# NSA's attention values: four heads at once, split values stationary, output transposed, probabilities scaled on GpSimd

## What is computed

```python
# per chunk of 128 tokens; 8 heads in 2 groups of R = 4; one group shares its keys and values
p_c = masked_softmax(q @ k_cmp - slope * dist)          # 31 compressed blocks
o_c = p_c @ v_cmp
s_s = q @ ks - slope * dist ; p_s = masked_softmax(s_s) # 8 blocks of 64 = all causal keys here
o_s = p_s @ vs
s_w = q @ kw - slope * dist ; p_w = masked_softmax(s_w) # window of 256
o_w = p_w @ vw
gc  = sigmoid(gate_logits)
o   = gc[0] * o_c + gc[1] * o_s + gc[2] * o_w
```

## Time and profile before

| | |
|---|---|
| median of 3 runs | 1001.13 us (1000.83 to 1001.33) |
| the profiled execution | 1001.37 us |
| its span in the trace | 999.5 us |
| PE busy in the span | 977.0 us (98%) |
| DVE, ACT, POOL busy | 568.5, 410.9, 141.4 us |
| NSA's attention slots | from 101.96 to 223.83 us |

### The profile page before, as it was taken

How to read it: one execution, slowest core, us unless ns; L and a number is a source line. 1 busy time by engine, 2 the same in 40 slices (tenths; PEclk the granted TensorE clock), 3 DMA queues, 4 the chain that set the end, 5 groups by cost and what they waited for, 6 DMA issues and landing times.

```text
span 999.5 us, 12861 instructions
## 1 busy us (share of the span) xinstructions
PE 977.0 (98%) x4869; PEld 812.6 (81%) x4869; DVE 568.5 (57%) x1162; ACT 410.9 (41%) x752; POOL 141.4 (14%) x185
## 2 busy tenths in 40 slices
PE   6999999999999999999999999999999999999998
PEld 5778788998888888888777788888888888888887
DVE  5747888863565885646555553575556556522113
ACT  5346555544246554445666433432232232221110
POOL 3000000010002112222434230022111112100000
PEclk9999999999999999999999999999999999999999
DMA  6512110103222211322101234222232223223222
GB/s 232 213 48 79 44 43 2 43 5 114 94 84 85 84 45 62 108 85 85 52 35 42 85 120 161 77 108 84 85 119 92 85 96 115 84 88 124 85 85 85
DMA packets 13693, 86.38 MB, mean 86 GB/s; under 512 B 1472, under 2 KB 1984, under 8 KB 4288
## 3 DMA queue, kind: packets, MB, share of 16 engines
q1 hardware_dynamic: 13632, 85.55, 23.7%
HBM read 83.44 MB, written 2.10 MB: 86 GB/s over the span
## 4 chain that ended last, share of the span: by engine, by line
PE 85%; DVE 8%; ACT 4%; issue 3%; DMA 1%; SPq 0%; DVEq 0%; ACTq 0%
PE ps L1429 22%; PE ps L1431 22%; PE ps L1430 22%; PE ps L1614 7%; PE ps L1457 3%; PE ps L1585 3%; DVE wl L938 2%; DVE prob L1148 1%; PE ps L1569 1%; PE ps L1570 1%; ACT prob_f L804 1%; DVE prob_f L1148 1%; PE ps L1484 1%; DVE pt_l L1170 1%; DMA x<-x 1%
## 5 line engine op out<-in xcount | busy, mean ns | idle before, releaser
L938 DVE TENSOR_TENSOR wl<-raw,wh 128x512 fp32r<-128x512 f32 (+2 forms) x118 | 172.0, 1462 | 130.6 <-ACT wh L644 129.0
L644 ACT ACTIVATE wh<-raw 128x2048 fp32r<-128x2048 f32 (+1 forms) x58 | 109.4, 1886 | 151.0 <-PE ps L1431 132.0
L1429 PE MATMUL ps<-aT_h,wh 128*128 128x512 f32 (+1 forms) x376 | 146.7, 390 | 0.9 <-DVE aT_l L947 0.9
L1430 PE MATMUL ps<-aT_l,wh 128*128 128x512 f32 (+1 forms) x376 | 146.4, 389 | 0.0
L1431 PE MATMUL ps<-aT_h,wl 128*128 128x512 f32 (+1 forms) x376 | 146.3, 389 | 0.0
L1429 PE MATMUL ps<-wh,aT_h 128*128 128x512 f32 x256 | 102.2, 399 | 0.0
L1431 PE MATMUL ps<-wh,aT_l 128*128 128x512 f32 x256 | 100.1, 391 | 0.0
L1430 PE MATMUL ps<-wl,aT_h 128*128 128x512 f32 x256 | 99.8, 390 | 0.0
L1429 PEld LDWEIGHTS ps<-aT_h,wh 128*128 128x128 f32 (+1 forms) x376 | 70.0, 186 | 16.6 <-issue 1.1
L1431 PEld LDWEIGHTS ps<-aT_h,wl 128*128 128x128 f32 (+1 forms) x376 | 70.0, 186 | 15.2
L1430 PEld LDWEIGHTS ps<-aT_l,wh 128*128 128x128 f32 (+1 forms) x376 | 70.0, 186 | 15.1
(11 more groups left out here) (234 smaller groups left out, 1774.2 us busy)
## 6 DMA issues: line engine op xcount, KB each, us to landing
raw<-wblk SPq DMA_DIRECT2D x72, 1024.0 KB, 4.8
x<-x SPq DMA_DIRECT2D x4, 512.0 KB, 5.5
w_sb<-w SPq DMA_DIRECT2D x1, 2048.0 KB, 9.2
hid<-x SPq DMA_DIRECT2D x1, 2048.0 KB, 9.0
out<-outt SPq DMA_DIRECT2D x8, 256.0 KB, 2.1
stage<-consts SPq DMA_DIRECT2D x1, 708.5 KB, 4.7
later<-consts SPq DMA_DIRECT2D x1, 448.0 KB, 5.4
par<-params SPq DMA_DIRECT2D x1, 204.5 KB, 8.6
```

The costliest lines, as they stand in the source:

```text
L644: nc.scalar.activation(wh[b % 2][:, 0:n], raw[b % RING][:, 0:n], ACT.Copy).then_inc(hi_ready, 4)
L938: ins = nc.vector.tensor_tensor(wl[b % RING][:, cols], raw[b % RING][:, cols], wh[b % 2][:, cols].bitcast(f32), ALU.subtract)
L1429: nc.tensor.matmul(dst, a_h, b_h, start=start, stop=False)
L1430: nc.tensor.matmul(dst, a_h, b_l, start=False, stop=False)
```

## The change

The 64 units of NSA are put in another order: by tile and group of four heads, four slc units and then four win units. Such four units share their values, so 128 keys of all four are handled in one step (kind, tile, group, key block); there are 38 steps.

- The probabilities live in a ring of 12 buffers (`prob_n`). DVE works out the coefficients for two units at a time, and GpSimd scales the probabilities in place before they are transposed.
- A step "TA" transposes the key block of four heads into one PSUM bank (four transpositions, as many as before in all). ACT writes the high part (`ptn_h`, 128x512), DVE the low part (`ptn_l`, 128x512). In place of these, the copies of probabilities out of PSUM and the sums into `otok` are gone.
- A step "VA" multiplies split values (`vn_hl`: high and low side by side, stationary) with the high and then the low part of the probabilities, moving, 512 columns each. It accumulates into one bank for each tile and group, into which the compressed part ("OC") writes first.
- "OX" adds the two halves of the bank (ACT copies one, DVE adds in two instructions), "OY" splits the tile's sum into `oT_h` and `oT_l`. The transpositions "OT" of NSA are gone.
- The compressed probabilities are split as well (`pcT`, `vc_hl`), and the values' low parts are written by DVE when the values are projected.

```diff
-        return [(k, h, 0, i) for i in range(TT) for h in range(8) for k in ("slc", "win")]
+        return [(k, 4 * g + r, 0, i) for i in range(TT) for g in range(2) for k in ("slc", "win") for r in range(4)]
+STEPS = [(q, kb) for q in range(16) for kb in range(group_of(q)[3])]
+PT_RING = 3
+P_RING = 12
-    t_lag, o_lag = {NSA: (2, 3), DIFF: (3, 5), FOX: (3, 5)}[m]
+    t_lag, o_lag = {NSA: (3, 7), DIFF: (3, 5), FOX: (3, 5)}[m]
...
+        for q in range(16):
+            kind, g, i, blocks = group_of(q)
+            end = 4 * q + 3
+            put(4 * q + 2, "C", 4 * q + 1)
+            put(4 * q + 4, "C", 4 * q + 3)
+            if kind == "slc":
+                put(end + t_lag + 1, "OC", i, g)
+            for kb in range(blocks):
+                n = STEPS.index((q, kb))
+                put(end + t_lag + kb, "TA", n)
+                put(end + t_lag + 2 + kb, "VA", n)
+            if kind == "win":
+                put(end + t_lag + 2 + blocks, "OX", i, g)
+                if g == 1:
+                    put(end + t_lag + 3 + blocks, "OY", i)
... ACT
+                    elif what == "TA":
+                        full(act, ("TA", j))
+                        if j >= PT_RING:
+                            step_read(act, j - PT_RING)
+                        nc.scalar.activation(ptn_h[j % PT_RING][:, :], ps[b][:, :], ACT.Copy).then_inc(ptn_hi, 1)
... DVE
-                                link(nc.vector.tensor_scalar(coef[:, j:j + 1], rl[:, j:j + 1], gsm[:, i, gi:gi + 1], None, ALU.mult))
+                                nc.vector.tensor_tensor(coef[:, j - 1:j + 1], rl[:, j - 1:j + 1], gsm[:, i, gi - 1:gi + 1], ALU.mult).then_inc(coef_ready, 1)
+                    elif what == "TA":
+                        dve.wait_ge(ptn_hi, j + 1)
+                        nc.vector.tensor_tensor(ptn_l[j % PT_RING][:, :], ps[b][:, :], ptn_h[j % PT_RING][:, :].bitcast(f32),
+                                                ALU.subtract).then_inc(psum_free[b], 1)
-                            nc.vector.scalar_tensor_tensor(dst, ps[b][:, 0:HD], coef[:, j:j + 1], dst, ALU.mult, ALU.add).then_inc(psum_free[b], 1)
... GpSimd
+            for j, u in enumerate(units_of(NSA)):
+                p = scores_at(NSA, j, span(u)[1])
+                pool.wait_ge(coef_ready, j // 2 + 1)
+                nc.gpsimd.tensor_scalar(p, p, coef[:, j:j + 1], None, ALU.mult).then_inc(pn_scaled, 1)
... PE
+                    elif what == "TA":
+                        if kb == 0:
+                            pe.wait_ge(pn_scaled, 4 * q + 4)
+                        transposes(("TA", j), [prob_n[(4 * q + r) % P_RING][:, kb * P:(kb + 1) * P] for r in range(4)])
+                    elif what == "VA":
+                        pe.wait_ge(ptn_hi, j + 1)
+                        nc.tensor.matmul(bk[:, :], v, ptn_h[j % PT_RING][:, :], start=False, stop=False)
+                        free(pe, ("TA", j))
+                        ins = nc.tensor.matmul(bk[:, :], v, ptn_l[j % PT_RING][:, :], start=False, stop=j in ENDS)
```

More of the change, by code:

```diff
@@ L93, in span, with group_of @@
     return s0, (i + 1) * P - s0
+def group_of(q):
+    kind, h, c, i = units_of(NSA)[4 * q]
+    return kind, h // 4, i, span(units_of(NSA)[4 * q])[1] // P
+STEPS = [(q, kb) for q in range(16) for kb in range(group_of(q)[3])]
+ENDS = [n for n, (q, kb) in enumerate(STEPS) if q % 2 and kb == group_of(q)[3] - 1]
+PT_RING = 3
+P_RING = 12
 GATE_STEPS = KD * 3
@@ L158, in attention_events @@
     for q in range(U):
-        if has_pv(m, q):
+        if m != NSA and has_pv(m, q):
             put(q + 1, "C", q)
@@ L172, in attention_events @@
             put(last + o_lag + 2, "OS", h // 2)
-    for i in range(TT if m != FOX else 0):
+    for i in range(TT if m == DIFF else 0):
         last = per * (i + 1) - 1 + o_lag
@@ L540, in bias_of, with step_read @@
             return (distW if kind == "win" else distD)[:, c0:c0 + n], SLOPES8[h if m == NSA else 2 * h + 1]
+        def step_read(eng, n):
+            if n in ENDS:
+                full(eng, ("ON", ENDS.index(n) // 2, ENDS.index(n) % 2))
+            else:
+                eng.wait_ge(step_done, n + 1 - sum(k <= n for k in ENDS))
         def scores_at(m, j, n):
+            if m == NSA:
+                return prob_n[j % P_RING][:, 0:n]
             return prob_f[j % TT][:, 0:n] if m == FOX else prob[:, j % 4, 0:n]
@@ L732, in compression @@
                     nc.scalar.activation(ksq[:, :], bank(("KC",))[0:HD, 0:HD], ACT.Square).then_inc(ksq_ready, 1)
+                    full(act, ("VC",))
+                    for a in range(4):
+                        rows = slice(32 * a, 32 * a + 32)
+                        ins = nc.scalar.activation(vc_hl[rows, a % 2, 0, :], bank(("VC",))[rows, 0:HD], ACT.Copy)
+                    ins.then_inc(vc_hi, 1)
                     act.wait_ge(kss_ready, 1)
@@ L1676, in _ @@
-                        bk = begin(("OC", j))
-                        for k in range(2):
-                            ins = nc.tensor.matmul(bk[:, 256 * k:256 * k + 256], pcT[:, k, :], vblk[:, :, :].rearrange("p a c -> p (a c)"),
-                                                   start=True, stop=True)
-                        done(("OC", j), ins)
-                    elif what == "OT":
-                        last = len(units) // TT * (j + 1) - 1
-                        if m == DIFF:
-                            pe.wait_ge(sub_ready, j + 1)
-                        else:
-                            free(pe, ("O", m, last - 1))
-                            free(pe, ("O", m, last))
+                        if e[2] == 0:
+                            free(pe, ("TC", j))
@@ L1695, in _ @@
                     cols = slice(c % 4 * P, c % 4 * P + P)
-                    if c == 0 and m < FOX:
+                    if c == 0 and m == NSA:
+                        pe.wait_ge(oTn_lo, TT)
+                    if c == 0 and m == DIFF:
                         free(pe, ("OT", m, TT - 2))
```

185 lines of the change are left out of this document (115 added, 70 removed).

## The result

The changed kernel takes 1026.62 us (median of 4 runs, 1025.09 to 1027.42), the kernel before 1001.1: a ratio of 1.0253, with a 95% interval of 1.0235 to 1.0271. It is slower, as forecast, but by 25.5 us and not by 13.9, and it lies above the range. The profiled execution took 1027.31 us, 25.9 more than that of before.

What follows compares the result with a forecast made beforehand. The prediction took a ring of four operations on DVE and ACT to bound NSA in place of PE: tiles of 135.9 against 121.9 us, so 1001.4 + 14.0 - 0.4 = 1015.0 us, range 1004 to 1023.

Steps and rivals of the forecast that it cites:

- PE is spared 16.9 us: NSA on PE: 14.4 us saved on values, 1.8 on output transpositions, 0.7 on the compressed part.
- The ring: NSA slots with a step: score, exponential, copy, subtraction in turn on DVE and ACT; 2.67 us at 512 keys, 2.42 at 384.
- The rival that PE stays the bound: Whole kernel: the ring does not bind, PE does and is faster, 985 us; chance 0.11.
- The sum by tile: NSA's tiles 0 to 3 and tail: 19, 30.5, 35.3, 42.6 and 8.5 us, together 135.9 against 121.9.
- The three other slots: Tile 3's slots without a step: 4.2 us, 2.6 of it the compressed part's own copy and subtraction.
- The waits for GpSimd: Scaling ahead of a group's first step: 1.4 us in tile 2, 1.6 in tile 1; bounds 0 to 6.
- the sign that the size is wrong: Tile 3: if PE's transpositions wait for GpSimd there as well, the forecast's size is wrong.
- the 19 for tile 0: NSA's tile 0, three steps: 19 us, taken between 16 and the 23 of the kernel before.
- 0 for the front: Ahead of NSA's scores: DVE's added subtractions (1.8 and 0.6 us) taken as net 0, bounds 0 to 0.5.
- the extras: Other operations inside the ring in NSA, 13 us: could be half hidden (-6) but not grow.
- The rival that it falls: PE waits so often that its granted clock falls; tile 3 and tail 76 us for 51, kernel 1040; chance 0.02.
- Contention of GpSimd and DVE: Weight splits beside GpSimd's scaling: by the row no cost; if splits in the ring doubled, 5 us, 1020.

Runs made afterwards that it cites:

- The opened loop: The change with only DVE's list reordered, each step's subtraction for ptn_l issued behind the next slot's score: 1010.21 us, 1.0088 to the kernel before.
- the fastest kernel: The change with tile 3's compressed transposition in banks 4 and 5, t_lag 4, PT_RING 4, VA/OX/OY a slot later, DVE's TA/TC/OX/OY operations behind the next score: 988.91 us.
- the kernel with the ring alone: The change with tile 3's compressed transposition in banks 4 and 5 and t_lag 4 in place of 3, DVE's order unchanged: 1016.62 us, 1.0151 to the kernel before.
- the bank edit: The change with tile 3's compressed transposition planned into banks 4 and 5 in place of bank 0: 1022.58 us, 1.0208 to the kernel before.

## Why the prediction was right in direction and wrong in size

**PE is spared 16.9 us.** Right, as far as it can be seen. In the fastest kernel PE's time in flight over the stage is 103.4 us, where my list had 105, and the whole kernel takes 988.9, where PE alone would have given 985. In the tail value matmuls stand 0.23 apart, and there are 76.

**The ring.** Right in mechanism. Handovers of FOX gave 2.67 and 2.42; measured were 2.66 and 2.42. The opened loop gave 16.4 us back. The rival that PE stays the bound failed at the place I had named for it: DVE's score does not start before the subtraction.

**The sum by tile.** Here the prediction failed. It gave 1015.0 and was 11.6 us too low, and by the runs the parts are:

- **"The three other slots: 4.2, of which 2.6 is the compressed part's own copy and subtraction behind an exponential."** I costed these two as operations in the ring and didn't ask who waits for the bank that they empty. PE's gate step does, 7.5 us long, for 4.0 us of the kernel's time. This is the step that failed outright. The two events stand in the same slot and their banks follow from the planner's one line on `spare`; the wait could be read before any run. In the kernel before, the same transposition stands in slot 40, where no gate chunk begins. With this wait gone the kernel took 1022.6, just inside the range.
- **The waits for GpSimd.** I gave them 3.0 us, and nothing in tile 3; measured 5.9, at the edge of my bounds (0 to 6), with PE waiting in tile 3 as well, which the prediction named as the sign that the size is wrong. This mis-sized the term by 2.9. A small part is the duration: I used 1.56 for a scaling of 512 keys, and the two in tile 3 at whose start a weight split runs take 2.1, which is 0.5 of one wait of PE. The rest isn't split up by the runs.
- **The ring itself.** Without GpSimd my sum gives 1012.0; the kernel with the ring alone took 1016.6, 4.6 more. 3.6 of it are tiles 0 to 2 (1.4, 1.1 and 1.1 by DVE's scores), where the 19 for tile 0 was a value between bounds. 0.7 is DVE's first score, at 103.53 and not at 102.87 as before, where I had taken 0 for the front. 0.9 is a slip of the sum: it adds up DVE's slots, which begin with DVE's first score (102.87 before), and sets them against 121.9 us that begin with PE's (101.96). Against that, tile 3 with its tail took 0.2 less than summed, and what lies behind the stage is 0.8 shorter, of which I had counted 0.4. In tile 1 one thing can be read: two output sums (OX) fall in its slots, and I counted one, at 0.75. The other stands in a slot without a step, where DVE waits for ACT's copy with nothing else to do, and this slot takes 2.73 where a plain one takes 0.66. Why tile 2 takes 1.1 us more, the runs don't separate.

4.0 + 2.9 + 4.6 = 11.5, of the 11.6 that were missing. The ring was the right mechanism, and yet its sum is the largest of the three errors.

**The bounds.** That the extras "could be half hidden (-6) but not grow" was right in its second half, and of those looked at none was hidden; but the range, which ended at 1023, had no room for a wait that I hadn't seen.

**The clock.** The rival that it falls came true as an event (0.86 to 0.91 in tiles 1 to 3) and failed as a price: one to three us, not 25. I had multiplied all of PE's work of tile 3 by two; it was at half clock for parts of it only. One such part is behind the long wait: from 199.82 to 202.94 PE issues three gate steps, two value matmuls and two of a score, 3.1 us where the same seven take 1.7 at the full clock, with DVE's score waiting for them. So by this estimate up to 1.4 us of what the bank wait cost came by way of the clock.

**Contention of GpSimd and DVE.** The prediction's reading that DVE isn't slowed holds: 685 against 687 ns. Its conclusion, that by the row contention costs nothing, doesn't: the row was of one side, and the other side, GpSimd, is held up. The price is small here, 0.5 us of one wait that can be pointed at.

## What to carry to other kernels

In a pipeline of engines with lists of their own, look for an operation that waits for another engine's result of the same step and stands ahead of the next step's first operation. Its wait is paid in every step. Move it behind the next step's first operation before counting what the instructions cost: here that alone was 16 us for the step's subtraction, then 10 more for the three other kinds of operation, while a deeper buffer brought 2.

For every moved result ask which bank it sits in and what is next to be written there, above all if a rule and not the author chose the bank. And give a slow helper engine a slot more: edits of order, bank, lag and buffers, and not one instruction fewer, turned a change that costs 2.5% into one that gains 1.2%.

## What the runs showed of the hardware

The granted clock of TensorE fell below 1.00 in three tiles of the change (0.89, 0.91 and 0.86). Short stretches of the change (us, PE busy, clock), around the long wait:

```profile
190.00:192.00 2.00, 2.00 (x13) 1.00 0.34 57
192.00:196.00 4.00, 0.30 (x3) 1.00 0.56 233
196.00:200.00 4.00, 0.18 (x1) 0.51 0.00 0
200.00:202.00 2.00, 2.00 (x5) 0.50 0.00 0
202.00:204.00 2.00, 2.00 (x8) 0.77 0.00 0
204.00:206.00 2.00, 2.00 (x15) 1.00 0.00 0
```

The clock is at 2.4 GHz in the first of the two idle stretches, at 1.2 GHz in the second and in the first two us of full work behind it, and full again from 204 on. It also fell without such a gap, and not in every execution. The change first, then the same place in the profile of the bank edit, whose list is the same up to tile 3 and which runs 0.87 us earlier there:

```profile
121.00:124.00 3.00, 1.62 (x6) 1.00 0.00 0
124.00:129.00 5.00, 5.00 (x24) 0.66 0.02 3
```
```profile
120.13:123.13 3.00, 1.64 (x6) 1.00 0.00 0
123.13:128.13 5.00, 4.74 (x26) 1.00 0.01 3
```

The longest wait ahead of a matmul is 0.67 us in the first and 0.66 in the second, and the work is the same; the clock fell in one and stayed in the other. What decided it, these profiles don't show.

GpSimd and DVE contend, and GpSimd pays. Over the 14 profiles, a GpSimd scaling of 128x512 takes 1.56 to 1.57 us (172 of them) where no weight split (DVE, two inputs in SBUF), output subtraction or `pc` step of DVE runs at its start. A split that begins more than 0.1 us after it doesn't change that (51 of the 172). Where a split is running at its start, or begins within 0.1 us of it, it takes 1.69 to 2.10 (34 of them). The two with an output subtraction at their start, which reads SBUF twice as well, take 1.63 and 1.66. At 128x384 it is 1.24 to 1.25 against 1.60 to 1.61, at 128x256 0.92 to 0.93 against 1.28 to 1.29. The splits themselves take 0.68 in the mean with nothing of GpSimd's beside them and 0.69 where they begin inside a GpSimd instruction.
